# Window attention in a fused encoder layer: score matmuls of two steps in one visit, transposed probabilities through one PSUM bank

## The reference

```python
def reference(x, ...):
    h = layer_norm(x, ln_in_g, ln_in_b)
    proj = h @ w_in[l]
    qa, ka, va, qb, kb, vb, ga, gb = jnp.split(proj, pts, axis=-1)
    ya = diff_attention(...)                      # branch A, 8 heads
    yb = window_attention(qb, kb, vb, ...)        # branch B, 16 query heads, 2 key heads
    merged = jax.nn.sigmoid(ga) * (ya @ w_branch_a[l]) + jax.nn.sigmoid(gb) * (yb @ w_branch_b[l])
    h = layer_norm(DEEPNORM_ALPHA * h + merged @ w_out[l], ln1_g[l], ln1_b[l])
    u = jnp.square(jax.nn.relu(h @ w_ff1[l]))
    return layer_norm(DEEPNORM_ALPHA * h + u @ w_ff2[l], ln2_g[l], ln2_b[l])

def window_attention(...):                        # 128 queries against a band of keys
    s = jnp.einsum('bnqgrd,bnkgd->bngrqk', qb, kb) * scale + bias
    s = jnp.where(mask[None, :, None, None], s, NEG_INF)
    m = jnp.maximum(jnp.max(s, axis=-1, keepdims=True), sink)
    e = jnp.exp(s - m)
    p = e / (jnp.sum(e, axis=-1, keepdims=True) + jnp.exp(sink - m))
    o = jnp.einsum('bngrqk,bnkgd->bnqgrd', p, vb)
```

## Time and profile before

| | before |
|---|---|
| median of 3 runs | 1788.44 us (1788.34 to 1789.07) |
| profiled execution | 1789.15 us |
| its span in the profile | 1787.2 us |
| TensorE busy | 1758.5 us, 98% |
| DVE, ACT, GpSimd busy | 1079.3, 741.7, 658.9 us |
| granted TensorE clock, mean | 0.999 |

### The profile page before, as it was taken

How to read it: one execution, slowest core, us unless ns; L and a number is a source line. 1 busy time by engine, 2 the same in 40 slices (tenths; PEclk the granted TensorE clock), 3 DMA queues, 4 the chain that set the end, 5 groups by cost and what they waited for, 6 DMA issues and landing times.

```text
span 1787.2 us, 25434 instructions
## 1 busy us (share of the span) xinstructions
PE 1758.5 (98%) x8815; PEld 1474.5 (83%) x8815; DVE 1079.3 (60%) x2358; ACT 741.7 (41%) x1592; POOL 658.9 (37%) x659
## 2 busy tenths in 40 slices
PE   6999999999999999999999999999999999999998
PEld 4888888888888888888888888788888888888886
DVE  6577777777665552013424654866666677777667
ACT  5566666666566665201321232322333332222232
POOL 4311112112134442232222340655566566555570
PEclk9999999999999999999999999999999999999999
DMA  5611111111211101134233430212111111211212
GB/s 177 211 36 49 33 49 37 49 38 45 47 39 34 33 25 36 48 118 142 94 95 118 130 107 1 83 58 60 47 47 47 47 47 58 60 47 47 73 33 95
DMA packets 143399, 117.91 MB, mean 66 GB/s; under 512 B 23556, under 2 KB 130252, under 8 KB 143308
## 3 DMA queue, kind: packets, MB, share of 16 engines
q1 hardware_dynamic: 134092, 112.52, 20.6%
q10 hardware_dynamic: 9216, 4.20, 0.8%
HBM read 99.88 MB, written 21.53 MB: 68 GB/s over the span
## 4 chain that ended last, share of the span: by engine, by line
PE 93%; DVE 3%; issue 1%; POOL 1%; ACT 1%; DMA 0%; SPq 0%; DVEq 0%; POOLq 0%; ACTq 0%
PE bank L594 27%; PE bank L596 27%; PE bank L595 27%; PE bank L620 4%; PE bank L699 4%; PE bank L682 2%; PE bank L631 1%; PE bank L683 1%; DMA res<-in_x_dram 0%; POOL y_lo L1317 0%; DVE small L1424 0%; ACT res L950 0%; POOL mix L1302 0%; DVE mix L1443 0%; ACT mix L1083 0%
## 5 line engine op out<-in xcount | busy, mean ns | idle before, releaser
L594 PE MATMUL bank<-hT_hi,w_hi 128*128 128x512 f32 x1296 | 513.4, 396 | 2.3 <-POOL hT_lo L1271 2.2
L596 PE MATMUL bank<-hT_hi,w_lo 128*128 128x512 f32 x1296 | 505.8, 390 | 0.0
L595 PE MATMUL bank<-hT_lo,w_hi 128*128 128x512 f32 x1296 | 505.0, 390 | 0.0
L1248 POOL TENSOR_TENSOR w_lo<-w_raw,w_hi 128x256 fp32r<-128x256 f32 x260 | 184.9, 741 | 585.5 <-ACT w_hi L900 585.5
L594 PEld LDWEIGHTS bank<-hT_hi,w_hi 128*128 128x128 f32 x1296 | 243.3, 188 | 55.0 <-POOL hT_lo L1271 3.9
L596 PEld LDWEIGHTS bank<-hT_hi,w_lo 128*128 128x128 f32 x1296 | 243.2, 188 | 52.2
L595 PEld LDWEIGHTS bank<-hT_lo,w_hi 128*128 128x128 f32 x1296 | 243.6, 188 | 47.4
L594 PE MATMUL bank<-y_hi 128*128 128x512 f32 (+1 forms) x548 | 205.9, 376 | 0.8 <-issue 0.8
L596 PE MATMUL bank<-y_hi,y_lo 128*128 128x512 f32 (+1 forms) x548 | 203.2, 371 | 0.0
L595 PE MATMUL bank<-y_lo,y_hi 128*128 128x512 f32 (+1 forms) x548 | 203.2, 371 | 0.0
L1337 POOL TENSOR_TENSOR y_lo<-y_full,y_hi 128x512 fp32r<-128x512 f32 x98 | 131.8, 1377 | 165.6 <-ACT y_hi L1183 165.6
(11 more groups left out here) (203 smaller groups left out, 2978.0 us busy)
## 6 DMA issues: line engine op xcount, KB each, us to landing
w_raw<-in_w_in_dram SPq DMA_DIRECT2D x100, 256.0 KB, 3.3
w_raw<-in_w_ff_dram SPq DMA_DIRECT2D x64, 256.0 KB, 4.1
y_full<-in_w_ff_dram SPq DMA_DIRECT2D x32, 512.0 KB, 3.8
bias_rows<-bias_line SPq DMA_DIRECT2D x3, 1536.0 KB
res<-in_x_dram SPq DMA_DIRECT2D x8, 512.0 KB, 7.4
x_spill<-res SPq DMA_DIRECT2D x8, 512.0 KB, 5.1
o_spill<-o_buf ACTq DMA_DIRECT2D x64, 64.0 KB, 1.6
w_raw<-in_w_branch_b_dram SPq DMA_DIRECT2D x16, 256.0 KB, 3.8
```

The source lines that it names most:

```text
L594: pe.matmul(bank, lhs[0], rhs[0], start=start, stop=False)
L595: pe.matmul(bank, lhs[0], rhs[1], start=False, stop=False)
L596: return pe.matmul(bank, lhs[1], rhs[0], start=False, stop=stop)
L1248: ins = pool.tensor_tensor(w_tile(n, 1)[:, at:at + 2], w_raw[:, at:at + 2, :], w_tile(n, 0)[:, at:at + 2].bitcast(F32), ALU.subtract)
```

## The change

From step 2 on the scores of two steps are issued together, in every even step: scores_b(s) and scores_b(s + 1), 24 matmuls in a row. Their four units need four banks, so the second of the two transposing banks joins the three score banks (SC_PAIRED). All batches of turned probabilities of branch B use the one bank that is left (tr_bank), and a batch waits until DVE has made the low part of the batch directly ahead of it. The two batches of a step are pulled apart: the first stands between the two halves of the projection piece, the second behind attend_b. On ACT and DVE the copies of the two batches are moved accordingly: in odd steps the first batch of step s - 1 is copied ahead of exp (ACT) and of the reciprocal (DVE), in even steps behind them; the q group's subtraction of DVE comes behind the first batch. Step 1 keeps its order on ACT and DVE.

```diff
--- before.py
+++ after.py
@@ -97,6 +97,12 @@
 SCORES = [("a", h, i, m, c) for h in range(A_HEADS) for i in range(NT) for c in range(1 + i // 4) for m in range(2)]
 SCORES += [("b", s // NT, s % NT, m, 0) for s in range(B_STEPS) for m in range(2)]
 SCORE = {s: n for n, s in enumerate(SCORES)}
+PAIRED = SCORE[("b", 0, 2, 0, 0)]
+
+
+def tr_bank(n):
+
+    return 0 if BATCH[("pb", 0, 0)] <= n <= BATCH[("pb", B_STEPS - 1, 1)] else n % 2
 
 
 def probs_count(n):
@@ -228,6 +234,12 @@
         banks = [ctx.enter_context(nc.psum_tensor(f"bank{i}", [P, HALF], F32)) for i in range(8)]
         GEMM, SC, TR, PV = banks[0:2], banks[2:5], banks[5:7], banks[7]
         TURN = TR + SC[1:3]
+        SC_PAIRED = SC + TR[1:2]
+
+        def score_bank(unit):
+
+            return SC_PAIRED[(unit - PAIRED) % 4] if unit >= PAIRED else SC[unit % 3]
+
         RING = [banks[2], banks[3], banks[4], banks[7]]
         RING8 = RING + [banks[5], banks[6], banks[0], banks[1]]
 
@@ -382,7 +394,7 @@
         def batch_views(batch, part):
 
             kind, n = batch[0], BATCH[batch]
-            bank = TR[n % 2][:, :].rearrange("p (n q) -> p n q", q=P)
+            bank = TR[tr_bank(n)][:, :].rearrange("p (n q) -> p n q", q=P)
             if kind == "pa":
                 _, h, i, b = batch
@@ -615,20 +627,19 @@
             def transposes(batch):
                 n = BATCH[batch]
                 if n >= 2:
-                    pe.wait_ge(tr_lo, n - 1)
+                    pe.wait_ge(tr_lo, n if tr_bank(n) == tr_bank(n - 1) else n - 1)
                 for at, src in probs_tiles(batch):
-                    mm = pe.transpose(TR[n % 2][:, at * P:(at + 1) * P], src, ident[:, :])
+                    mm = pe.transpose(TR[tr_bank(n)][:, at * P:(at + 1) * P], src, ident[:, :])
                 mm.then_inc(tr_done, 1)
 
             def scores(units, pieces):
 
-                if units[1] >= 3:
-                    pe.wait_ge(scores_read, units[1] - 2)
+                pe.wait_ge(scores_read, (units[0] - PAIRED) // 4 * 4 + PAIRED if units[0] >= PAIRED else units[1] - 2)
                 for queries, keys, at in pieces:
                     for left, right in ((0, 0), (0, 1), (1, 0)):
                         for m in range(2):
                             rows = slice(m * HD, (m + 1) * HD)
-                            mm = pe.matmul(SC[units[m] % 3][:, at:at + keys.stop - keys.start], queries[left][rows],
+                            mm = pe.matmul(score_bank(units[m])[:, at:at + keys.stop - keys.start], queries[left][rows],
                                            k_b[right][rows, keys], start=not (left or right), stop=left == 1)
                             if left == 1 and at == pieces[-1][2]:
                                 mm.then_inc(scores_done, 1)
@@ -721,8 +732,8 @@
                                 pe.wait_ge(freed_act, freed(True, LAST[TILE[("va", h)]]))
                                 for b in range(2):
                                     transposes(("va", h, b))
-            def group_b(piece):
-                group(*ORDER[B_GROUP + piece // 2], range(piece % 2 * 4, piece % 2 * 4 + 4))
+            def group_b(piece, kts=range(4)):
+                group(*ORDER[B_GROUP + piece // 2], range(piece % 2 * 4 + kts[0], piece % 2 * 4 + kts[-1] + 1))
 
             def scores_b(s):
                 g, i = s // NT, s % NT
@@ -733,9 +744,10 @@
                        [([t[:, half, j, at:at + P] for t in q_b], slice(i * P - CHUNK if i else 0, (i + 1) * P), j * 192 + (0 if i else CHUNK))
                         for j in range(2)])
 
-            def transposes_b(s):
-                pe.wait_ge(pb_scaled, s + 1)
-                for b in range(2 if s % NT else 1):
+            def transposes_b(s, b):
+                if b == 0:
+                    pe.wait_ge(pb_scaled, s + 1)
+                if b == 0 or s % NT:
                     transposes(("pb", s, b))
 
             def attend_b(s):
@@ -754,8 +766,13 @@
                 mm.then_inc(pv_done, 1)
 
             for s in range(B_STEPS):
-                if s != 1:
+                if s == 0:
+                    scores_b(0)
+                elif s % 2 == 0:
+                    if s == 2:
+                        pe.wait_ge(tr_lo, BATCH[("vb", 0, 1)] + 1)
                     scores_b(s)
+                    scores_b(s + 1)
                 if s == 0:
                     group_b(0)
                     scores_b(1)
@@ -771,13 +788,17 @@
                     for b in range(2):
                         transposes(("vb", 0, b))
                 if s < B_STEPS - 1:
-                    group_b(s + 1)
-                transposes_b(s - 1)
+                    group_b(s + 1, range(2))
+                transposes_b(s - 1, 0)
+                if s < B_STEPS - 1:
+                    group_b(s + 1, range(2, 4))
                 if s >= 2:
                     attend_b(s - 2)
+                transposes_b(s - 1, 1)
             group(TILE[("gb", 1)], 0)
-            transposes_b(B_STEPS - 1)
+            transposes_b(B_STEPS - 1, 0)
             attend_b(B_STEPS - 2)
+            transposes_b(B_STEPS - 1, 1)
             group(TILE[("gb", 1)], 1)
             attend_b(B_STEPS - 1)
@@ -1071,12 +1092,14 @@
                 act.wait_ge(pv_done, A_HEADS * NT + s + 1)
                 act.activation(res[:, 2 * g:2 * g + 2, i * P:(i + 1) * P], PV[:, 0:2 * P].rearrange("p (j q) -> p j q", j=2), ACT.Copy).then_inc(ob_read, 1)
 
-            def probs_hi(s):
-                for b in range(2 if s % NT else 1):
+            def probs_hi(s, b):
+                if b == 0 or s % NT:
                     batch_hi(("pb", s, b))
 
             for s in range(B_STEPS):
                 slot, first = s % 2, 0 if s % NT else CHUNK
+                if s % 2 and s > 1:
+                    probs_hi(s - 1, 0)
                 act.wait_ge(max_ready, A_HEADS * NT + s + 1)
                 act.wait_ge(sink_set, s + 1)
                 for c in range(4):
@@ -1087,6 +1110,8 @@
                     for b in range(2):
                         batch_hi(("pa", A_HEADS - 1, NT - 1, b))
                     out_rows(A_HEADS * NT - 2, A_HEADS - 1, NT - 2)
+                if s % 2 == 0 and s:
+                    probs_hi(s - 1, 0)
                 if s == 1 or s % 2 == 0 and 2 <= s < B_STEPS - 4:
                     group_hi(*ORDER[B_GROUP + s // 2])
                 if s == 1:
@@ -1098,9 +1123,10 @@
                 if s >= B_STEPS - 2:
                     act.wait_ge(yb_lo, 1)
                     gate_raw(TILE[("gb", 0)], s - (B_STEPS - 2))
-                if s >= 1:
-                    probs_hi(s - 1)
+                if s == 1:
+                    probs_hi(0, 0)
                 if s >= 2:
+                    probs_hi(s - 1, 1)
                     o_rows_b(s - 2)
                 if s % NT in (1, 3):
@@ -1594,8 +1621,8 @@
                                 batch_lo(("va", h, b))
                             qk_lo(*late)
                             late = None
-            def probs_lo(s):
-                for b in range(2 if s % NT else 1):
+            def probs_lo(s, b):
+                if b == 0 or s % NT:
                     batch_lo(("pb", s, b))
 
@@ -1629,20 +1656,29 @@
                     for b in range(2):
                         batch_lo(("pa", A_HEADS - 1, NT - 1, b))
                     sum_halves(A_HEADS * NT - 2)
-                if s == 1 or s % 2 == 0 and 2 <= s < B_STEPS - 4:
-                    qk_lo(*ORDER[B_GROUP + s // 2])
+                if s == 1:
+                    qk_lo(*ORDER[B_GROUP])
+                elif s % 2:
+                    probs_lo(s - 1, 0)
                 dve.wait_ge(exp_done, A_HEADS * NT + s + 1)
                 dve.reciprocal(inv4[:, slot, :], sums4[:, slot, :]).then_inc(inv_ready, 1)
+                if s % 2 == 0 and s:
+                    probs_lo(s - 1, 0)
+                    if s < B_STEPS - 4:
+                        qk_lo(*ORDER[B_GROUP + s // 2])
                 if s == 1:
                     sum_halves(A_HEADS * NT - 1)
                     for b in range(2):
                         batch_lo(("vb", 0, b))
-                if s >= 1:
-                    probs_lo(s - 1)
+                if s == 1:
+                    probs_lo(0, 0)
+                if s >= 2:
+                    probs_lo(s - 1, 1)
                 if s == B_STEPS - 3:
                     yb_low(0)
             yb_low(1)
-            probs_lo(B_STEPS - 1)
+            for b in range(2):
+                probs_lo(B_STEPS - 1, b)
 
             def gated(kind, c, half, dst):
 
```

More of the change, by code:

```diff
@@ L392, in batch_views @@
                 width = 512 if b == 0 else 256
-                return [(pT_b[s % 2][part][:, 512 * b:512 * b + width], TR[n % 2][:, 0:width])]
+                return [(pT_b[s % 2][part][:, 512 * b:512 * b + width], TR[tr_bank(n)][:, 0:width])]
             if kind == "va":
@@ L1110, in _ @@
             split_weights(TILE[("gb", 2)])
-            probs_hi(B_STEPS - 1)
```

(4 more changed lines are left out.)

## The result

| | before | after |
|---|---|---|
| median of 20 runs | 1788.73 us (1787.85 to 1790.48) | 1791.07 us (1790.07 to 1792.68) |
| ratio | | 1.0013, 95% interval 1.0007 to 1.0018 |
| profiled execution, span | 1789.15, 1787.2 us | 1791.92, 1790.1 us |

The change makes the kernel slower, by 0.13%: less than the 0.2% that the prediction set as its bound, and 3.4 us away from the predicted 1787.7. In the two profiles branch B itself, from the first score matmul of step 1 to the first matmul of attend_b(31) (called **the stretch** from here), takes 187.71 us before (501.67 to 689.38) and 189.39 after (502.49 to 691.89): 1.7 us longer. Another 0.8 us of the profiled difference stands ahead of step 1, where nothing was changed; there single executions differ anyway (step 1 starts between 501.10 and 502.49 in the thirteen profiles of this case).

A forecast was written before the change was run, and what follows sets the result against it. TensorE, busy 1758.5 of 1787.2 us, was taken as the bound. Saved 5.3, less 1.4 (head), 2.9 (tail) and 0.3 (body), gave 0.7 us gained: 1787.7 us, range 1785.0 to 1791.0, no change that can be told.

The forecast's parts named there:

- 15 visits fewer: TensorE in branch B: each visit to the scores costs 0.37 us on the way in and out; 15 fewer save 5.5 us.
- other changes of kind: TensorE, two more switches between kinds of matmul in each step: 0.01 us a pair of steps, at most 0.08 a change.
- head: Step 1: TensorE waits 1.6 us instead of 0.3 before the first probabilities, with six projection matmuls ahead; cost 1.4 us.
- body: Ordinary pairs: neg_max slowed by GpSimd's weight split stalls the second batch about 0.1 in three pairs; 0.3 us, bounds 0 and 4.
- tail: Last steps: four waits for DVE's copies, 1.4, 1.05, 0.55 and 0.5, less the 0.6 there now; cost 2.9 us.
- T1: Second batch of a step's transposes in the timetable; wants the bank at 5.89 us into a pair, with 0.2 of slack left.
- is over by then: Head: the new wait for bank 6 (second value batch, some 516.2 us) is past before step 2's scores at 516.7.
- The clock: Granted clock assumed to stay at 1.00, the upper of two levels (2.4 GHz).
- free ends: Case where first and last steps of branch B cost nothing: time would be 1783.1 us.
- Rival 3: neg_max meets the wrong piece of GpSimd's split in eight pairs, 0.35 each: 2.8 us, 1790.2 us; chance 0.12.
- Rival 2: Slower by the single bank: copy chain 0.5 longer makes the second batch 0.3 late in 15 pairs, 4.5 us, 1792.2; chance 0.14.
- Rival 1: Ends of branch B cost little: 1785.8 us with the last steps at 1 us, 1783 to 1784 with both nearly free; chance 0.17.

The follow-up runs named there:

- run 8: The moves of run 5, run 6 and run 7 together on the changed kernel; 1785.49 us, ratio 0.9980 to the kernel before.
- run 9: run 8's kernel without the pairing, scores of every step at its own start again; 1790.78 us, ratio 1.0011 to the kernel before.
- run 7: Changed kernel with run 4's edit, and DVE also subtracts the first batch ahead of the reciprocal in even steps; 1789.15 us, ratio 0.9999.
- run 5: Changed kernel, but GpSimd's weight split waits until neg_max of the next step is made; 1790.64 us, ratio 1.0007 to the kernel before.
- run 1: Changed kernel with step 1's projection piece whole again ahead of the first probabilities; 1791.49 us, ratio 1.0014 to the kernel before.
- run 2: Changed kernel with yb_low(0) moved into DVE's gap ahead of the reciprocal in step 29; 1789.25 us, ratio 1.0001 to the kernel before.
- run 6: Changed kernel with run 2's move, and the first whole projection group dealt out between the last steps' batches; 1787.67 us, ratio 0.9990.
- run 4: Changed kernel with the first batch's high copy in the middle of ACT's exps in even steps, on ACT alone; 1792.73 us, ratio 1.0019.
- run 3: Changed kernel without the joint visit, scores of each step at its own start; 1804.5 us, ratio 1.0084 to the kernel before.
- run 10: run 8's kernel with step 1's whole piece and scores_b(2) ahead of the first probabilities, scores_b(3) in step 2; 1784.41 us, ratio 0.9974.
- run 11: run 10's kernel, but GpSimd's first weight split no longer waits for neg_max; 1785.21 us, ratio 0.9979 to the kernel before.

## Why the prediction was wrong

Its terms beside what the runs gave, in us of the stretch (plus is longer):

| step | forecast | measured | from |
|---|---|---|---|
| 15 visits fewer | -5.5 | -5.3 | runs 8 and 9 |
| other changes of kind | +0.15 | +0.5 | pairs of run 9 and before |
| head | +1.4 | +1.4 | S(1) to S(2) 15.04, before 13.64 |
| body | +0.3 | +1.9 | run 7 against after |
| tail | +2.9 | +3.1 | run 8 against after 3.7, less the 0.6 of the earlier trace rows |
| sum | -0.7 | +1.6 | 1.7 measured |

**The step that failed is the body**, "T1 then stalls about 0.1 in those three: 0.3 us in all"; 1.9 us were measured. Two things were wrong in it. First, the text took the pairs behind a step with i = 0 as 0.15 shorter for neg_max's due time, but not that T1 itself comes 0.36 earlier there, since attend_b has six matmuls: that uses the whole slack of 0.26 before neg_max adds anything. neg_max itself did there what was forecast, 0.45 to 0.47 us, 0.3 above its plain time; so 0.36 + 0.3 - 0.26 = 0.4, in three pairs 1.2, and without neg_max's part about 0.1 in the first pair. Second, steps 20/21: there DVE starts the reductions 1.42 after the first score matmul (613.55, 614.97) and not 1.06. That was to be read in the trace of before:

```profile
613.27 0.36 PE L631 MATMUL bank<-y_hi 64*128 64x192 f32 x2
...
614.68 0.36 DVE L1620 CUSTOM_DVE_ANT_0 mix<-bank,bias_b_buf 128x192 f32<-128x192 f32 x1 [0.30 <-issue]
```

It is 1.41 there too, and in every other trace of this case. With neg_max's 0.60 it makes 0.36 + 0.44 - 0.26 = 0.54 (0.57 measured). What holds DVE for those 0.35 us in this one step stayed open. The prediction took one pair's timetable for all; where the slack is 0.2, the deviations of single pairs are the whole term. Runs 5 and 7 show both sides: without the shared wait 1.33 come back, with the copies' order changed 1.9.

**The saving** was right in its price, 0.37 from four rows of one visit against 0.352 over 15. The price of the other changes of kind was put too low, 0.01 a pair instead of 0.03.

**The head** was right in place, size and releaser (1.40 of idle <-DVE). Left out was what stands behind it: run 1 shows that with the piece left whole bank 6 and DVE's copies would have taken 1.0 of the 1.4 us, and neg_max under GpSimd's split the rest. The remark that the wait for bank 6 "is over by then" holds only because TensorE waited already.

**The tail** had its four waits, 1.4, 1.05, 0.55 and 0.5; measured they are 1.3, 1.25, 0.6 and 0.6. yb_low took 1.89 under GpSimd's product as worked out.

**The clock** was assumed at 1.00 throughout. In the profile after it is; in several of the others it is not (below), and of the twenty runs after the change eleven have a mean clock of 0.998 and nine one of 0.999, with medians of 1791.62 and 1790.74. The 96 runs of before beside the eleven kernels all have 0.999. That lifts the median of after by about 0.3 us above that of its runs at 0.999, and with it just over the end of the range.

**The whole miss** of 3.4 us is then 2.4 in the stretch (0.7 less was forecast, 1.7 more measured), 0.3 from the baseline (the median of before is 1788.73 in twenty runs, 1788.44 in the three that the forecast started from), about 0.3 from the clock, and some 0.4 that no row accounts for. A slip of the text changed nothing in it: with free ends its own terms give 1787.7 - 1.4 - 2.9 = 1783.4, not 1783.1.

**The rivals.** Rival 3 named the right pair of engines, but in eight pairs at 0.35; it was three pairs and steps 20/21. Rival 2's single bank is the mechanism all the same: everything lost in body and tail is a batch waiting for the copy of the one ahead of it. Rival 1, cheap ends, is refuted: the head cost 1.4 us, and runs 2 and 6 got back from the tail just what it was said to cost. Its support was misread, too: the earlier trace rows has ACT busy for 25.70 of 40.00 us, nearer two thirds than half.

## What to carry to other kernels

A saving repeated 15 times is easy to size from one visit; what it runs into is not. When the slack left by a new order is a few tenths, put the timetable of every kind of step beside it (here the steps with fewer matmuls, and each single pair's start of the reductions), since the exceptions pay and the ordinary pair does not. And a buffer given away costs where the cover ends: at the head and the tail, work has to be dealt out between the hand-overs (run 6), and the copies placed so that the released buffer is not behind unrelated work (runs 2 and 7); then the same pairing gained 0.2% instead of losing 0.13%. What the moves alone would give the kernel with two banks was not run; the one wait that it has in the tail is 0.6 us.

## What was not expected of the hardware

After the waits of the tail the granted clock can fall. Windows of run 1's profile:

```profile
675.00:676.00 1.00, 0.77 (x7) 0.80 (x8) 1.00 (x8) 0.10 (x1) 0.00 (x0) 0.99 0.02 8
676.00:677.00 1.00, 1.00 (x7) 1.00 (x7) 0.83 (x4) 1.00 (x4) 0.00 (x0) 0.50 0.00 0
677.00:678.00 1.00, 1.00 (x6) 1.00 (x6) 0.22 (x1) 1.00 (x5) 0.00 (x0) 0.50 0.00 0
```

and TensorE's timeline ahead of and in it:

```profile
673.77 0.44 PE L632 MATMUL bank<-ident,mix 128*128 128x128 f32 x2 [1.17 <-DVE y_lo L1424]
675.23 0.63 PE L632 MATMUL bank<-ident,mix 128*128 128x128 f32 x4 [1.02 <-DVE y_lo L1424]
...
676.30 0.42 PE L607 MATMUL bank<-y_lo,y_hi 128*128 128x256 f32 x1
676.52 0.41 PE L608 MATMUL bank<-y_hi,y_lo 128*128 128x256 f32 x1
```

The clock is at its lower level, 1.2 GHz, though TensorE is busy throughout; the matmuls stand 0.21 us apart instead of 0.12, and the stretch is 190.35, 0.95 longer than after's although S(4) stands at 25.58 in both and the order is the same from there on. The profiles of runs 4, 5 and 7 show it too (0.83 to 0.86 as mean of 670 to 680 us). In after the same waits of 1.17 and 1.02 left it at 1.00 in the profiled execution. In run 3's profile it stayed at 1.00 behind a wait of 1.83, though 2 of its 5 runs have a mean clock of 0.998. The single waits of 1.23 and 1.40 in step 1 left the clock at 1.00 in every profile. The kernels whose tail has no wait of 1.17 us or more (runs 2, 6, 8, 9, 10, 11) have a mean clock of 0.999 in all 66 runs; in runs 1, 4, 5 and 7 it is 0.998 in 27 of 44. So short waits can cost more than their own length, but not in each execution; what decides it in the single one stayed open.
